# Up-projection of a feed-forward layer: plain weight blocks split by ScalarE and VectorE, and three plain pairs in place of four ahead of the seven-product pairs

## The chip, the cores and the metric

One core of a Trainium2 chip runs the whole program. The metric is device time in microseconds (us), the median of the runs of one kernel. Its engines work side by side, each through its own queue in order, and meet at semaphores: TensorE (PE) multiplies, VectorE (DVE), ScalarE (ACT) and GpSimd (POOL) work elementwise, SyncE (SP) issues the DMA transfers.

## The reference

Two layers of a model with 1024 channels over 1040 positions (16 meta tokens and 1024 tokens). The change lies in the feed-forward part of the first:

```
xn = rms_norm(h, ffn_pre_g)                       # 1024 channels
gu = xn @ w_up                                    # 1024 x 5632
g  = causal_dwconv(gu[..., :2816], w, b)          # 3 taps
f  = (gelu(g) * gu[..., 2816:]) @ w_down          # 2816 -> 1024
h  = h + rms_norm(f, ffn_post_g)
```

All of it is float32. The columns of `w_up` are cut into 22 blocks of 128 gate columns and 22 of 128 up columns; a gate block and its up block are a pair.

## The kernel before

**Numbers.** Every float32 factor is split into two float16 parts, high and low; weights are first multiplied by 64 (`WSCALE`). One product is three matmuls: high by high, high by low, low by high. To split a weight block of 128x1024 means to make `hi = f16(64 w)` and `lo = 64 w - hi`.

**The phase.** `ffn_up_phase` makes the 22 pairs. The first `PLAIN` = 4 are plain: the gate block (even number b, buffer slot 0) and the up block (odd, slot 1) are each multiplied over three token tiles of 342 and eight blocks of channels, 72 matmuls a block, into banks 0 to 2 and 3 to 5 of PSUM. The first two blocks are made ahead; their last token tile waits for the norm that ends the phase before. The other `WINO` = 18 pairs take seven products of half the size instead of eight (Strassen's scheme in Winograd's form), over two token parts of 257 and 256: 7 x 2 x 4 x 3 = 168 matmuls a pair. These need sums of the input blocks, T1 to T4, and sums of the weight blocks, S1 to S4.

**The input sums.** They are made while the plain pairs run, in eight rounds (`T_ROUNDS`), one after another through the same four float32 buffers. A round r is: four additions on POOL (`whole_inputs(r)`, L2191), which wait until the round before has been split; four differences on DVE (`t_differences(r)`, L2469); four casts to the high part on ACT (`t_highs(r)`, L2351); four subtractions for the low part on DVE (L2472). The second product of the first seven-product pair needs all rounds.

**The plain weight blocks** from number 2 on: SP loads one when the slot's last low part is made; ACT multiplies it by 64 in place (`weight_scaled`, L2333), ACT casts it to the high part (`weight_high`, L2357), POOL subtracts (`low_part`, L2179). PE starts a block when its low part is there (`L.cut`) and its PSUM banks are emptied (`L.emptied`).

**A plain pair q after its matmuls:** ACT copies the gate banks out (L2387), DVE convolves (three instructions, L2483 to L2485), ACT takes the gelu (L2372), DVE multiplies by the up banks (L2514, semaphore `s_f`, which empties them), ACT and DVE split the result (`f_high`, L2377; `f_low`, L2491).

**The order** on each engine is written out by hand. In the loop over the four plain pairs DVE has: a round, the convolution, another round, the multiplication by the up banks, `f_low`. For the last plain pair the first two weight quarters of seven-product pair 0 take the place of the second round: ACT makes `high(0, "A11")` and `high(0, "A12")` (L2368), DVE the low parts (L2476). PE's order for seven-product pair 0 is the product of A11 (P1), then a wait for `s_f` of the last plain pair, then the product of A12 (P2), then that of S2 (P6), and four more. POOL makes S1 to S4 (`combine`, L2201 to L2209) after the last round's additions.

After the 22 pairs PE goes on with the down-projection, whose unit u takes PSUM bank `u % 6`.

Of the kernel before, what the change touches and what calls it, by code (L numbers as in the profile page):

```python
# [10 lines left out]
ALU = mybir.AluOpType  # L11
# [238 lines left out]
def done(L, b):  # L250

    return b * L.parts + (L.parts + SLOTS)
# [1811 lines left out]
    return nc.tensor.matmul(out, lo, xhi, start=False, stop=(j == DB - 1))  # L2064


PLAIN = 4
WINO = FFB - PLAIN
SPLITS = ("A11", "A12", "A22", "S1", "S2", "S3", "S4")
PRODUCTS = ("P1", "P2", "P6", "P5", "P7", "P4", "P3")  # L2070
# [4 lines left out]
PART_W = (257, 256)  # L2075
PART_AT = (0, 2 * PART_W[0])
F_STEPS = 2 * PARTS
T_ROUNDS = PARTS * (DB // 2)
Z_PARKED = slice(META, META + 755)
Z_FIRST = slice(META, F0 + 2 * FT)  # L2080
Z_LAST = slice(F0 + 2 * FT, META + 755)
# [2 lines left out]
def ffn_up_phase(nc, S, L, Ld, hs, ssq, rows, parked_z):  # L2084
# [3 lines left out]
    with Phase(nc) as ctx:  # L2088
# [32 lines left out]
        s_hi, s_lo = ({n: sem(f"{n}_{part}") for n in SPLITS} for part in ("hi", "lo"))  # L2121
        s_p = sem("wino_products")
        s_p1, s_u2, s_u3, s_c11, s_c12, s_c22 = (sem(n) for n in ("p1", "u2", "u3", "c11", "c12", "c22"))
        s_zp, s_whole, s_whigh, s_third = sem("z_parked"), sem("weights_scaled"), sem("weights_high"), sem("third_part")
        half = lambda x, i: x[:, i * BANK:(i + 1) * BANK]
        s32 = {"A11": half(L.raw[:, 0, :], 0), "A12": half(L.raw[:, 0, :], 1), "A21": half(L.raw[:, 1, :], 0), "A22": half(L.raw[:, 1, :], 1),
               "S1": half(rows, 0), "S2": half(rows, 1), "S3": half(L.raw[:, 0, :], 0), "S4": half(L.raw[:, 0, :], 1)}
# [8 lines left out]
        with nc.Block() as block:  # L2136
# [36 lines left out]

            @block.gpsimd
            def _(pool):
                def low_part(b):
                    s = b % SLOTS
                    pool.wait_ge(s_whigh, b - SLOTS + 1)
                    nc.gpsimd.tensor_tensor(L.lo[:, s, :], L.raw[:, s, :], L.hi[:, s, :], ALU.subtract).then_inc(L.cut, 1)  # L2179

                def whole_inputs(r):
                    e, j = divmod(r, DB // 2)
                    if r == 0:
                        pool.wait_ge(C.summed, 1)
                    else:
                        pool.wait_ge(s_tlo, 4 * r)
                    if r == DB // 2:
                        pool.wait_ge(C.low, DB)
                        pool.wait_ge(s_zp, 32)
                    for t, (k, h) in zip(temps_of(r), ((j, 1), (j, 0), (j + DB // 2, 1), (j + DB // 2, 0))):  # L2190
                        nc.gpsimd.tensor_tensor(t, S.xhi[:, k, x_at(e, h)], S.xlo[:, k, x_at(e, h)], ALU.add).then_inc(s_tsum, 1)  # L2191

                def combine(i):
                    pool.wait_ge(s_in["U"], 16 * (i + 1))
                    pool.wait_ge(s_in["A11"], 16 * (i + 1))
                    if i == 0:
                        pool.wait_ge(s_tlo, 4 * (DB // 2))
                    else:
                        pool.wait_ge(s_lo["S1"], i)
                        pool.wait_ge(s_lo["S2"], i)  # L2200
                    nc.gpsimd.tensor_tensor(s32["S1"], s32["A21"], s32["A22"], ALU.add).then_inc(s_comb, 1)  # L2201
                    pool.wait_ge(s_comb, 4 * i + 1)
                    nc.gpsimd.tensor_tensor(s32["S2"], s32["S1"], s32["A11"], ALU.subtract).then_inc(s_comb, 1)
                    pool.wait_ge(s_comb, 4 * i + 2)
                    pool.wait_ge(s_lo["A11"], i + 1)
                    nc.gpsimd.tensor_tensor(s32["S3"], s32["A11"], s32["A21"], ALU.subtract).then_inc(s_comb, 1)
                    pool.wait_ge(s_in["A12"], 16 * (i + 1))
                    pool.wait_ge(s_lo["A12"], i + 1)
                    nc.gpsimd.tensor_tensor(s32["S4"], s32["A12"], s32["S2"], ALU.subtract).then_inc(s_comb, 1)  # L2209

                for b in range(SLOTS, SLOTS * PLAIN):
                    whole_inputs(b - SLOTS)
                    if b == SLOTS * PLAIN - 1:
                        whole_inputs(b - SLOTS + 1)
                    low_part(b)
                whole_inputs(T_ROUNDS - 1)
                for i in range(WINO):
                    combine(i)
                pool.wait_ge(s_p, free(WINO - 1, "A12"))
                cut_first(nc, S, pool, Ld, 1)  # L2220
                pool.wait_ge(s_p, free(WINO - 1, "A22"))
                cut_first(nc, S, pool, Ld)

            @block.tensor
            def _(pe):
# [87 lines left out]
                for part in range(PARTS_AHEAD):  # L2313
                    k0, k1 = DOWN_PARTS[part]
                    pe.wait_ge(Ld.cut, part + 1)
                    pe.wait_ge(s_flo, 2 * k1)
                    for k in range(k0, k1):
                        hi, lo = (x[:, part, (k - k0) * P:(k - k0 + 1) * P] for x in (Ld.hi, Ld.lo))
                        fhi, flo = (x[0][:, k, :] for x in (S.f_hi, S.f_lo))
                        out = S.ps[:, 0, :]  # L2320
                        nc.tensor.matmul(out, hi, fhi, start=(k == 0), stop=False)
                        nc.tensor.matmul(out, hi, flo, start=False, stop=False)
                        nc.tensor.matmul(out, lo, fhi, start=False, stop=False)

            @block.scalar
            def _(act):
                nc.scalar.sem_inc(L.emptied, SLOTS)
                nc.scalar.preload_act_table_set("natural_log_exp_and_others")

                def weight_scaled(b):  # L2330
                    s = b % SLOTS
                    act.wait_ge(L.landed[s], 16 * (b // SLOTS + 1))
                    nc.scalar.activation(L.raw[:, s, :], L.raw[:, s, :], ACT.Copy, scale=WSCALE).then_inc(s_whole, 1)  # L2333

                link_root(nc, S, act, C, 0, DB)
                for k in range(DB):
                    link_square(nc, act, C, k)
                weight_scaled(2)
                link_root(nc, S, act, C, 1, DB)
                for k in range(DB):  # L2340
                    link_high(nc, act, C, k)
# [10 lines left out]

                def weight_high(b):
                    s = b % SLOTS
                    act.wait_ge(s_whole, b - SLOTS + 1)
                    act.wait_ge(L.products, b + 1)
                    nc.scalar.activation(L.hi[:, s, :], L.raw[:, s, :], ACT.Copy).then_inc(s_whigh, 1)  # L2357

                def high(i, name):
                    if name[0] == "A":  # L2360
# [20 lines left out]

                for q in range(PLAIN):
                    if q:
                        t_highs(2 * q + (q + 1 == PLAIN))
                    act.wait_ge(L.products, done(L, q * 2))
                    act.wait_ge(s_conv, q)
                    nc.scalar.activation(fm(raw[:, :]), psum_tn(S, 0)[:, :, 0:FT], ACT.Copy, scale=1.0 / WSCALE).then_inc(s_raw, 1)  # L2387
# [2 lines left out]
                    if q + 1 < PLAIN:  # L2390
                        weight_high(2 * q + 2)
                    if q == 0:
                        t_highs(0)
                        weight_scaled(3)
                        weight_high(3)
                    elif q + 1 < PLAIN:
                        weight_scaled(2 * q + 3)
                    if q + 1 == PLAIN:
                        for name in ("A11", "A12"):
                            high(0, name)  # L2400
                    gelu(q)
                    if q + 1 < PLAIN:
                        t_highs(2 * q + 1)
                    if q + 2 < PLAIN:
                        weight_scaled(2 * q + 4)
                    if q + 1 == PLAIN:
                        for name in ("S1", "S2"):
                            high(0, name)
# [2 lines left out]
                    if 0 < q < PLAIN - 1:  # L2411
                        weight_high(2 * q + 3)
                    f_high(q)
                    if q + 2 == PLAIN:
                        t_highs(2 * q + 2)
                for i in range(WINO):
                    q = PLAIN + i
                    for e in range(PARTS):
# [35 lines left out]
            def _(dve):  # L2454
# [19 lines left out]
                def low(i, name):  # L2474
                    dve.wait_ge(s_hi[name], i + 1)
                    nc.vector.scalar_tensor_tensor(w16[1][name], s32[name], WSCALE, w16[0][name], ALU.mult, ALU.subtract).then_inc(s_lo[name], 1)  # L2476
# [19 lines left out]
                def gated(i, q):  # L2496
                    dve.wait_ge(s_gelu, q + 1)
                    for e in range(PARTS):
                        dve.wait_ge(s_p, made(i, "P4", e))
                        for h, (of, scale) in enumerate(((bank_a(i, e), 1.0 / WSCALE), (c22[e], 1.0))):  # L2500
                            nc.vector.scalar_tensor_tensor(f_at(acc, e, h), of, scale, f_at(acc, e, h), ALU.mult, ALU.mult).then_inc(s_f, 1)

                for q in range(PLAIN):
                    t_differences(2 * q + (q + 1 == PLAIN))
                    dve.wait_ge(s_raw, q + 1)
                    convolve(q)
                    if q + 1 < PLAIN:
                        t_differences(2 * q + 1)
                    else:
                        low(0, "A11")  # L2510
                        low(0, "A12")
                    dve.wait_ge(L.products, done(L, q * 2 + 1))
                    dve.wait_ge(s_gelu, q + 1)
                    nc.vector.scalar_tensor_tensor(fm(acc[:, :]), psum_tn(S, 1)[:, :, 0:FT], 1.0 / WSCALE, fm(acc[:, :]),  # L2514
                                                   ALU.mult, ALU.mult).then_inc(s_f, F_STEPS)
                    if q + 1 == PLAIN:
                        for name in ("S1", "S2"):
                            low(0, name)
                    f_low(q)
                    if q + 2 == PLAIN:  # L2520
                        t_differences(2 * q + 2)
                for name in ("S3", "A22", "S4"):
                    low(0, name)
                for i in range(WINO):
# [81 lines left out]
def ffn_down_phase(nc, S, A, Lz, Ld, L, down, ssq, parked_h, s_parked_h, parked_z):  # L2606
# [7 lines left out]
    with Phase(nc) as ctx:  # L2614
# [21 lines left out]
        with nc.Block() as block:  # L2636
# [24 lines left out]
            def _(pe):  # L2661
                f_of = lambda parts, k, r: parts[2][:, k, :] if r else parts[k // F_KEPT][:, k % F_KEPT, :]

                def part(u, q):
                    i = LOAD_OF[u, q]
                    at, w = toks(u).start, width(u)
                    out = S.ps[:, u % 6, 0:w]
                    k0, k1 = DOWN_PARTS[q]
                    pe.wait_ge(s_cut, i + 1)
                    for k in range(k0, k1):  # L2670
# [28 lines left out]
            def _(act):  # L2699
# [9 lines left out]
                def evac(u):  # L2709

                    act.wait_ge(s_pr, NQ * u + NQ)
                    w = width(u)
                    ps = S.ps[:, u % 6, 0:w]
                    nc.scalar.activation(down[:, DOWN_UNITS[u][0], toks(u)], ps, ACT.Copy, scale=1.0 / WSCALE)
                    if not new_sum(u) and u >= 2:
                        act.wait_ge(s_acc, sums_by(u - 2))
# [1522 lines left out]
```

## Time and profile before

| | |
|---|---|
| median of 3 runs | 2248.89 us (2245.49 to 2254.71) |
| profiled execution | 2248.3 us, of it the span of the trace 2246.5 us |
| mean granted TensorE clock | 0.989 of full speed |
| PE busy | 2141.7 us, 95% of the span |
| DVE, ACT, POOL busy | 1577.0 us (70%), 1008.3 us (45%), 631.7 us (28%) |
| plain blocks 2 to 7 on PE | from 953.79 us to 1020.5 us of the span |
| seven-product pairs on PE | from 1025.80 us to 1359.97 us |

In the rows of a timeline the first number is the start in us from the start of the span, the second the time from the first start to the last end; x3 says that three like instructions are merged. In brackets stand the idle time of the engine before it and what ended it. A matmul's own duration is a model (they overlap); the distance of two starts is what PE takes for one.

### The profile page before, as it was taken

To read this page: it belongs to the slowest core of one execution; us is meant where nothing else is said; L and a number is where in the kernel's file an instruction comes from. 1 tells how busy PE (TensorE), PEld (TensorE's weight loads), DVE (VectorE), ACT (ScalarE), POOL (GpSimd) and SP (SyncE) were. 2 spreads that over 40 slices of the span, in tenths; PEclk is the share of its full clock that TensorE was granted. 3 is DMA by queue.
4 is the path that set the end of the run, shared out by engine and by line. 5 is a ranking of instruction groups with operands and counts; after the bars stand their busy time and mean duration, and the time that the engine had idled before them with its cause. 6 is when DMAs were issued, how large, how long until landed. Compare 5 with 4: busy or idle time off the path is not lost. (4 is left out here: it accounts for less than half of the span.)

```text
span 2246.5 us, 45705 instructions
## 1 busy us (share of the span) xinstructions
PE 2141.7 (95%) x19060; PEld 1435.6 (64%) x19060; DVE 1577.0 (70%) x2075; ACT 1008.3 (45%) x1778; POOL 631.7 (28%) x405
## 2 busy tenths in 40 slices
PE   7999999999999899898999999999999999989998
PEld 4666665556666566567888885458644445578847
DVE  7966888988888656777888884257687675236654
ACT  3227776666666444544444443235553332224321
POOL 4556763200011120053333321000155532101160
PEclk9999999999999999999999999999999999999999
DMA  3113213777777521211111115326433522033412
GB/s 137 48 47 105 85 63 84 138 139 147 143 137 148 135 100 63 100 44 64 58 57 57 58 43 184 103 71 211 131 99 118 177 91 89 11 99 100 169 62 76
DMA packets 292085, 224.25 MB, mean 100 GB/s; under 512 B 205536, under 2 KB 255904, under 8 KB 290480
## 3 DMA queue, kind: packets, MB, share of 16 engines
q1 hardware_dynamic: 291888, 221.44, 35.5%
q8 instruction: 146, 2.39, 0.4%
q14 instruction: 51, 0.42, 0.1%
HBM read 148.46 MB, written 28.86 MB: 79 GB/s over the span
## 5 line engine op out<-in xcount | busy, mean ns | idle before, releaser
L1543 DVE TENSOR_TENSOR_SCAN att_left<-att_left,att_unseen_prefix 16x16 f32<-16x16 f32 (+5 forms) x144 | 183.5, 1275 | 35.0 <-ACT att_left L1382 35.0
L3027 PE MATMUL ps<-second_x_hi,whi_z 128*128 128x512 f16 (+1 forms) x480 | 178.8, 372 | 3.4 <-POOL wlo_z L2992 1.9
L1276 PE MATMUL ps<-x_hi,whi_z 128*128 128x348 f16 x560 | 175.6, 314 | 3.4 <-DVE att_q L1487 3.4
L3029 PE MATMUL ps<-second_x_hi,wlo_z 128*128 128x512 f16 (+1 forms) x480 | 178.5, 372 | 0.0
L3028 PE MATMUL ps<-second_x_lo,whi_z 128*128 128x512 f16 (+1 forms) x480 | 178.5, 372 | 0.0
L1278 PE MATMUL ps<-x_hi,wlo_z 128*128 128x348 f16 x560 | 174.6, 312 | 0.0
L1277 PE MATMUL ps<-x_lo,whi_z 128*128 128x348 f16 x560 | 174.4, 311 | 0.0
L2992 POOL TENSOR_TENSOR wlo_z<-wraw_z,whi_z 128x1024 f16<-128x1024 f32 x28 | 65.8, 2348 | 180.0 <-ACT whi_z L3220 180.0
L1502 DVE SCALAR_TENSOR_TENSOR att_left_split<-att_left,att_left_split 128x256 f16<-128x256 f32 (+7 forms) x128 | 107.0, 836 | 7.4 <-ACT att_left_split L1396 7.3
L1382 ACT ACTIVATE att_left<-ps 16x16 f32<-16x16 f32 (+5 forms) x144 | 86.1, 598 | 39.7 <-PE ps L1292 39.5
L1396 ACT ACTIVATE att_left_split<-att_left 128x256 f16<-128x256 f32 (+7 forms) x128 | 86.7, 678 | 36.2 <-DMA att_left_turned<-att_left_split 29.4
L3220 ACT ACTIVATE whi_z<-wraw_z 128x1024 f16<-128x1024 f32 x28 | 29.6, 1056 | 132.4 <-PE ps L3029 117.3
L1323 PE MATMUL ps<-att_left_turned,att_v_tokens 128*64 128x128 f16 x1728 | 63.4, 227 | 25.7 <-DMA att_left_turned<-att_left_split 18.2
L1234 POOL CAST att_v_meta_split<-att_v_meta 32x128 f16<-32x128 f32 x8 | 9.2, 1152 | 277.4 <-ACT att_v_meta L1388 277.4
L3027 PEld LDWEIGHTS ps<-second_x_hi,whi_z 128*128 128x128 f16 x480 | 46.9, 98 | 62.5 <-issue 6.3
L2254 PE MATMUL ps<-x_hi,whi_z 128*128 128x257 f16 (+1 forms) x288 | 79.1, 275 | 5.3 <-DVE wlo_z L2476 5.3
L1323 PEld LDWEIGHTS ps<-att_left_turned,att_v_tokens 128*64 128x64 f16 x1728 | 53.3, 114 | 44.4 <-issue 34.8
L1276 PEld LDWEIGHTS ps<-x_hi,whi_z 128*128 128x128 f16 x560 | 54.5, 97 | 42.1 <-issue 14.7
L3028 PEld LDWEIGHTS ps<-second_x_lo,whi_z 128*128 128x128 f16 x480 | 47.0, 98 | 53.4 <-issue 3.6
L219 PE MATMUL ps<-x_hi,whi_xbc 128*128 128x348 f16 x240 | 74.6, 311 | 6.8 <-DVE x_lo L529 5.9
L3029 PEld LDWEIGHTS ps<-second_x_hi,wlo_z 128*128 128x128 f16 x480 | 47.0, 98 | 53.2
L2255 PE MATMUL ps<-x_lo,whi_z 128*128 128x257 f16 (+1 forms) x288 | 79.0, 274 | 0.0
(695 smaller groups left out, 6703.6 us busy)
## 6 DMA issues: line engine op xcount, KB each, us to landing
wraw_z<-in_w_second SPq DMA_DIRECT2D x30, 512.0 KB, 3.6
wraw_z<-in_w_up SPq DMA_DIRECT2D x26, 512.0 KB, 3.6
wraw_z<-in_w_qkv SPq DMA_DIRECT2D x24, 512.0 KB, 4.5
wraw_z<-in_w_down SPq DMA_DIRECT2D x20, 512.0 KB, 3.7
raw_down<-in_w_down SPq DMA_DIRECT2D x20, 512.0 KB, 3.5
seg<-dt_a_sums SPq DMA_DIRECT2D x18, 512.0 KB, 5.1
wraw_z<-in_w_up SPq DMA_DIRECT2D x36, 256.0 KB, 2.5
second_work<-parked_units SPq DMA_DIRECT2D x7, 1280.0 KB, 6.0
```

The costliest lines, as they stand in the source:

```text
L1276: nc.tensor.matmul(lin_ps(g), hi, xhi, start=(kb == 0), stop=False)
L1277: nc.tensor.matmul(lin_ps(g), hi, xlo, start=False, stop=False)
L1278: last = nc.tensor.matmul(lin_ps(g), lo, xhi, start=False, stop=(kb == DB - 1))
L1323: nc.tensor.matmul(o_ps(n)[half(a)], vt[:, t.p % 2, (NSTEP - 1) * (x + 1) - t.j + m, half(a)], turned[t.slot][:, keys_at(t, a) + y * t.j + ...
L1382: nc.scalar.activation(of_head(t, a, 0, t.wide), z_ps(a)[0:t.rows, 0:t.wide], ACT.Sigmoid, scale=-0.125).then_inc(s_keep, 1)
L1396: last = nc.scalar.activation(left_part(e, 0, P * t.j), of_head(t, a, 0, P * t.j), ACT.Copy, scale=PSCALE)
L1502: last = nc.vector.scalar_tensor_tensor(low_, of_head(t, a, 0, P * t.j), PSCALE, high, ALU.mult, ALU.subtract)
L1543: nc.vector.tensor_tensor_scan(x, x, unseen, 1.0, ALU.mult, ALU.max).then_inc(s_scan, 1)
L2254: nc.tensor.matmul(out, hi, xhi, start=first and j == 0, stop=False, skip_group_check=True)
L3027: nc.tensor.matmul(out, hi, xhi, start=(j == 0), stop=False)
L3028: nc.tensor.matmul(out, hi, xlo, start=False, stop=False)
L3029: return nc.tensor.matmul(out, lo, xhi, start=False, stop=(j == DB - 1))
```

## The change

It does four things. (1) `PLAIN` is 3 and `WINO` 19. (2) The split of plain blocks moves: ACT makes `hi = f16(64 raw)` in one instruction, DVE makes `lo = 64 raw - hi` in one (`plain_low`); the scaling in place and POOL's subtraction are gone. (3) The eight rounds are spread over three plain pairs by the table `T_AT`: for each pair what comes ahead of the convolution, what after it, and what after `f_low`. (4) The PSUM banks of the down-projection are turned by two when `WINO` is odd.

```diff
-PLAIN = 4
+PLAIN = 3
 WINO = FFB - PLAIN
...
+def down_bank(u):
+    return (u + 2 * (WINO % 2)) % 6
+
+
 T_ROUNDS = PARTS * (DB // 2)
+T_AT = (((0,), (1,), (2,)), ((3,), (4,), (5,)), ((6,), (7,), ()))
...
@@ block.gpsimd
-                for b in range(SLOTS, SLOTS * PLAIN):
-                    whole_inputs(b - SLOTS)
-                    if b == SLOTS * PLAIN - 1:
-                        whole_inputs(b - SLOTS + 1)
-                    low_part(b)
-                whole_inputs(T_ROUNDS - 1)
+                for r in range(T_ROUNDS):
+                    whole_inputs(r)
...
@@ block.scalar
                 def weight_high(b):
                     s = b % SLOTS
-                    act.wait_ge(s_whole, b - SLOTS + 1)
+                    act.wait_ge(L.landed[s], 16 * (b // SLOTS + 1))
                     act.wait_ge(L.products, b + 1)
-                    nc.scalar.activation(L.hi[:, s, :], L.raw[:, s, :], ACT.Copy).then_inc(s_whigh, 1)
+                    nc.scalar.activation(L.hi[:, s, :], L.raw[:, s, :], ACT.Copy, scale=WSCALE).then_inc(s_whigh, 1)
...
                 for q in range(PLAIN):
                     if q:
-                        t_highs(2 * q + (q + 1 == PLAIN))
+                        for r in T_AT[q][0]:
+                            t_highs(r)
...
                     if q == 0:
-                        t_highs(0)
-                        weight_scaled(3)
+                        for r in T_AT[q][0]:
+                            t_highs(r)
                         weight_high(3)
-                    elif q + 1 < PLAIN:
-                        weight_scaled(2 * q + 3)
...
                     gelu(q)
-                    if q + 1 < PLAIN:
-                        t_highs(2 * q + 1)
-                    if q + 2 < PLAIN:
-                        weight_scaled(2 * q + 4)
+                    for r in T_AT[q][1]:
+                        t_highs(r)
...
@@ block.vector
+                def plain_low(b):
+                    s = b % SLOTS
+                    dve.wait_ge(s_whigh, b - SLOTS + 1)
+                    nc.vector.scalar_tensor_tensor(L.lo[:, s, :], L.raw[:, s, :], WSCALE, L.hi[:, s, :], ALU.mult, ALU.subtract).then_inc(L.cut, 1)
+
                 for q in range(PLAIN):
-                    t_differences(2 * q + (q + 1 == PLAIN))
+                    for r in T_AT[q][0]:
+                        t_differences(r)
+                    if q + 1 < PLAIN:
+                        plain_low(2 * q + 2)
                     dve.wait_ge(s_raw, q + 1)
                     convolve(q)
-                    if q + 1 < PLAIN:
-                        t_differences(2 * q + 1)
-                    else:
+                    if q == 0:
+                        plain_low(3)
+                    if q + 1 == PLAIN:
                         low(0, "A11")
                         low(0, "A12")
+                    for r in T_AT[q][1]:
+                        t_differences(r)
                     dve.wait_ge(L.products, done(L, q * 2 + 1))
                     dve.wait_ge(s_gelu, q + 1)
                     nc.vector.scalar_tensor_tensor(fm(acc[:, :]), psum_tn(S, 1)[:, :, 0:FT], 1.0 / WSCALE, fm(acc[:, :]),
                                                    ALU.mult, ALU.mult).then_inc(s_f, F_STEPS)
+                    if 0 < q < PLAIN - 1:
+                        plain_low(2 * q + 3)
...
                     f_low(q)
-                    if q + 2 == PLAIN:
-                        t_differences(2 * q + 2)
+                    for r in T_AT[q][2]:
+                        t_differences(r)
```

## Rows read from the trace of the kernel before

**Rows 1.** The page, busy time by engine (share of the span, instructions)

```profile
PE 2141.7 (95%) x19060; PEld 1435.6 (64%) x19060; DVE 1577.0 (70%) x2075; ACT 1008.3 (45%) x1778; POOL 631.7 (28%) x405
```

**Rows 2.** Who PE waited for, 1026 to 1365 us: total, times, longest

```profile
PE ps L2254 <- ACT mixed_squares L2380: 0.4, 1, 0.4
```

**Rows 3.** Timeline of PE at the seams of the phase

```profile
952.26 0.31 PE L2064 MATMUL ps<-x_hi,wlo_z 128*128 128x342 f16 x1
953.79 0.31 PE L219 MATMUL ps<-x_hi,whi_z 128*128 128x342 f16 x1 [1.22 <-POOL wlo_z L2179]
...
964.10 0.31 PE L221 MATMUL ps<-x_hi,wlo_z 128*128 128x342 f16 x1
966.39 0.32 PE L219 MATMUL ps<-x_hi,whi_z 128*128 128x342 f16 x1 [1.99 <-ACTq L2410]
...
1020.18 0.31 PE L221 MATMUL ps<-x_hi,wlo_z 128*128 128x342 f16 x1
1025.80 0.37 PE L2254 MATMUL ps<-x_hi,whi_z 128*128 128x257 f16 x1 [5.31 <-DVE wlo_z L2476]
...
1029.70 0.27 PE L2254 MATMUL ps<-x_hi,whi_z 128*128 128x257 f16 x1
...
1046.11 0.27 PE L2254 MATMUL ps<-x_hi,whi_z 128*128 128x257 f16 x1
...
1359.97 0.38 PE L2321 MATMUL ps<-second_x_hi,whi_z 128*128 128x512 f16 x1
```

**Rows 4.** Busy time of PE by stretch: length, busy, granted clock, DMA

```profile
968.00:970.00 2.00, 2.00 (x9) 0.50 0.00 0
...
1026.00:1028.00 2.00, 2.00 (x11) 0.50 0.01 4
```

**Rows 5.** Timeline of DVE, 920 to 1026 us

```profile
920.81 1.22 DVE L1989 SCALAR_TENSOR_TENSOR wlo_z<-wraw_z,whi_z 128x1024 f16<-128x1024 f32 x1
...
951.78 2.15 DVE L2472 TENSOR_TENSOR t<-mixed_squares,t 128x257 f16<-128x257 f32 x1 [1.49 <-ACT t L2351]
...
954.86 0.80 DVE L2483 TENSOR_SCALAR gate_conv<-gate_raw,params 128x1024 f32<-128x1024 f32 x1
...
957.31 1.58 DVE L2485 SCALAR_TENSOR_TENSOR gate_conv<-gate_raw,params,gate_conv 128x1024 f32<-128x1024 f32 x1
...
965.07 1.22 DVE L2514 SCALAR_TENSOR_TENSOR gate_conv<-ps,gate_conv 128x1026 f32<-128x1026 f32 x1
...
967.68 1.16 DVE L2491 TENSOR_TENSOR f_lo_other<-gate_conv,f_hi_other 128x512 f16<-128x512 f32 x1
968.77 1.34 DVE L2469 TENSOR_TENSOR mixed_squares<-mixed_squares 128x257 f32<-128x257 f32 x3
...
971.49 0.42 DVE L2472 TENSOR_TENSOR t<-down_squares,t 128x257 f16<-128x257 f32 x1
...
1016.40 3.34 DVE L2469 TENSOR_TENSOR mixed_squares<-mixed_squares 128x256 f32<-128x256 f32 x3 [2.66 <-POOL z L2191]
...
1021.12 0.42 DVE L2472 TENSOR_TENSOR z<-z 128x256 f16<-128x256 f32 x1
1021.60 0.81 DVE L2483 TENSOR_SCALAR gate_conv<-gate_raw,params 128x1024 f32<-128x1024 f32 x1
...
1024.97 1.28 DVE L2476 SCALAR_TENSOR_TENSOR wlo_z<-wraw_z,whi_z 128x512 f16<-128x512 f32 x2
```

**Rows 6.** Timeline of POOL, 951 to 1020 us

```profile
951.51 2.13 POOL L2179 TENSOR_TENSOR wlo_z<-wraw_z,whi_z 128x1024 f16<-128x1024 f32 x1 [22.77 <-ACT whi_z L2357]
955.02 4.40 POOL L2191 TENSOR_TENSOR mixed_squares<-x_hi,x_lo 128x257 f32<-128x257 f16 x3 [1.38 <-DVE t L2472]
959.38 0.67 POOL L2191 TENSOR_TENSOR down_squares<-x_hi,x_lo 128x257 f32<-128x257 f16 x1
...
1013.81 1.92 POOL L2191 TENSOR_TENSOR mixed_squares<-x_hi,x_lo 128x256 f32<-128x256 f16 x3 [4.28 <-DVE z L2472]
...
1016.32 1.26 POOL L2201 TENSOR_TENSOR down_squares<-wraw_z 128x512 f32<-128x512 f32 x1
```

**Rows 7.** Timeline of ACT, 970 to 974 us

```profile
970.93 1.01 ACT L2387 ACTIVATE gate_raw<-ps 128x1026 f32<-128x1026 f32 x1
972.11 1.06 ACT L2357 ACTIVATE whi_z<-wraw_z 128x1024 f16<-128x1024 f32 x1 [0.17 <-ACT gate_raw L2387]
```

More of the change, by code:

```diff
@@ L2123, in ffn_up_phase @@
         s_p1, s_u2, s_u3, s_c11, s_c12, s_c22 = (sem(n) for n in ("p1", "u2", "u3", "c11", "c12", "c22"))
-        s_zp, s_whole, s_whigh, s_third = sem("z_parked"), sem("weights_scaled"), sem("weights_high"), sem("third_part")
+        s_zp, s_whigh, s_third = sem("z_parked"), sem("weights_high"), sem("third_part")
         half = lambda x, i: x[:, i * BANK:(i + 1) * BANK]
@@ L2175, in _ @@
             def _(pool):
[L2176 to L2179, printed above, removed]
                 def whole_inputs(r):
@@ L2319, in _ @@
                         fhi, flo = (x[0][:, k, :] for x in (S.f_hi, S.f_lo))
-                        out = S.ps[:, 0, :]
+                        out = S.ps[:, down_bank(0), :]
                         nc.tensor.matmul(out, hi, fhi, start=(k == 0), stop=False)
@@ L2328, in _ @@
                 nc.scalar.preload_act_table_set("natural_log_exp_and_others")
[L2330 to L2333, printed above, removed]
                 link_root(nc, S, act, C, 0, DB)
@@ L2337, in _ @@
                     link_square(nc, act, C, k)
-                weight_scaled(2)
                 link_root(nc, S, act, C, 1, DB)
@@ L2413, in _ @@
                     f_high(q)
-                    if q + 2 == PLAIN:
-                        t_highs(2 * q + 2)
+                    for r in T_AT[q][2]:
+                        t_highs(r)
                 for i in range(WINO):
@@ L2519, in _ @@
                     f_low(q)
-                    if q + 2 == PLAIN:
-                        t_differences(2 * q + 2)
+                    for r in T_AT[q][2]:
+                        t_differences(r)
                 for name in ("S3", "A22", "S4"):
@@ L2666, in part @@
                     at, w = toks(u).start, width(u)
-                    out = S.ps[:, u % 6, 0:w]
+                    out = S.ps[:, down_bank(u), 0:w]
                     k0, k1 = DOWN_PARTS[q]
@@ L2712, in evac @@
                     w = width(u)
-                    ps = S.ps[:, u % 6, 0:w]
+                    ps = S.ps[:, down_bank(u), 0:w]
                     nc.scalar.activation(down[:, DOWN_UNITS[u][0], toks(u)], ps, ACT.Copy, scale=1.0 / WSCALE)
```

## The prediction

> **What bounds the kernel now.** I read the page first: PE is busy for 95% of the span [rows 1], so time is won where PE has less to do or stops waiting, and nowhere else. The question is then how near PE each part of this phase runs. The waits of PE during the seven-product pairs answer for these: one of 0.4 us in more than 300 us [rows 2]. So they run at PE's pace, and their price is a distance of starts: from the second pair's first matmul at 1046.11 to the end at 1359.97 are 313.86 us for 17 pairs, 18.46 us a pair, 0.1099 us for each of 168 matmuls [rows 3]. A plain block is 72 matmuls; block 2 runs from 953.79 and issues its last at 964.10, which is 71 steps of 0.1452 us [rows 3]: 10.46 us a block, 20.9 us a pair.
>
> The timeline of PE at the seams shows where it stands still between 952.6 and 1026 us: 1.22 us ahead of block 2, for POOL's low part; 1.99 us ahead of block 3, for its PSUM banks, which ACT hands over after DVE's multiplication; 5.31 us ahead of seven-product pair 0, for DVE's low part of A11 [rows 3]. The stretches of clock say what follows the longer two: the granted clock is 0.50, the 1.2 GHz level, at 968 to 970 and at 1026 to 1028 us [rows 4]. Blocks 3 to 7 take from 966.39 to 1020.33 (the last start and a step), 53.9 us where five blocks at full clock are 52.3: 1.6 us lost. The product of A11 takes from 1025.80 to 1029.70, 3.90 us where 24 x 0.1099 = 2.64 are due: 1.26 us lost [rows 3].
>
> The last of those waits tells who sets the pace here. It isn't PE: it is the chain of rounds on POOL and DVE, with the convolutions between them. That chain has eight rounds to fit whether there are four plain pairs or three, and the timelines of DVE and POOL price its links.
>
> - A round on DVE with POOL quiet or nearly so: 968.77 to 971.91, 3.15 us. The last round, beside POOL's first sum of weights: 1016.40 to 1021.54, 5.1 us [rows 5].
> - The four additions on POOL: 1013.81 until the next instruction at 1016.32, 2.55 us; beside a convolution 955.02 to 960.05, 5.0 us [rows 6].
> - A convolution: 1021.60 until the low parts at 1024.97, 3.4 us; beside the additions 954.86 to 958.89, 4.0 us [rows 5].
> - The multiplication 1.2 us; `f_low` 1.8 us with the wait of 0.8 us ahead of it left out (the second half is seen stretched to 1.16); a low part of 128x1024 on DVE, in the phase before, 1.22 us [rows 5].
> - ACT: the copy of the gate banks starts 2.16 us after the start of a round that stands ahead of it, the high part of the next block 1.18 us after the copy, for 1.06 us [rows 5, 7].
>
> **The change part by part.**
>
> *The pair.* One plain pair, 20.9 us of PE, becomes one seven-product pair, 18.46 us: 2.5 us less on PE. SP moves the same bytes for it. The bank turn of the down-projection adds no instruction.
>
> *ACT.* Six scalings and two high parts fall away. ACT is idle for much of this stretch, so this is worth something only at one place: block 4's high part, which now needs no scaling ahead of it. Nothing on PE waits for that today. I take 0.
>
> *POOL.* Six subtractions go, 2.1 us or more each (951.51, 2.13 us) [rows 6]. They lengthened the chain in two ways. They kept POOL from the next additions, and they held DVE: its L2472 that began at 951.78 took 2.15 us, ending at 953.93 just after POOL's 953.64, where the like one at 971.49 took 0.42 [rows 5, 6].
>
> *DVE.* Four low parts come in, 4 x 1.22 us, all on the chain. What they do shows only in order, so I walk it, from 948.48 us, where DVE starts round 0 in both kernels:
>
> 1. Round 0 is free of POOL: the low parts follow ACT's casts, end 953.15 (954.94 before). Low part of block 2: 954.4. PE starts block 2 at 954.55, 0.75 us later than before.
> 2. Convolution 0 beside round 1's additions: 958.4. Low part of block 3: 959.65. Round 1: 962.9. Multiplication: 964.2. PE ends block 2 at 965.0 and goes straight on: the wait of 1.99 us and its slow clock (1.6 us) are gone.
> 3. Wait 0.8 and `f_low` 1.8: 966.8. Round 2: 969.95. Round 3's additions start only now and DVE has nothing else in its queue: 972.55. Round 3: starts there; the copy of gate 1 is queued behind its casts on ACT, 972.55 + 2.16 + 1.18 + 1.06 = 976.95 for block 4's high part, low part at 978.25. PE ends block 3 at 975.5 and starts block 4 at 978.4: a **new wait of 2.9 us**, perhaps with a slow clock after it.
> 4. Convolution 1 (its additions mostly done, 3.7): 981.95. Round 4: 985.1. Multiplication: 986.3. High part 5 on ACT and low part on DVE: 988.7. PE ends block 4 at 988.9 and meets it with 0.2 us in hand. `f_low`: 990.0. Round 5: 993.15. Additions of round 6, again with nothing beside them: 995.75. Round 6 and the copy behind its casts: 999.0.
> 5. PE ends block 5 at 999.3, or at about 1001 if the clock fell in step 3. That doesn't matter: convolution 2, 4.0 us, ends at 1003.0 and the low part of A11 at 1003.7. PE starts pair 0 at 1003.85, after a wait of 4.5 us (5.31 before), again at the low clock: A11 ends at 1007.75.
> 6. Here is the second new wait. The low part of A12 ends at 1004.3, and round 7 now stands **between it and the multiplication of the last plain pair**, while POOL already combines weights, as it did beside the last round before: 5.1 us, 1009.4. Multiplication: 1010.6. PE, which needs these banks for A12, starts it at 1010.75 and has waited 3.0 us. The copies, S1, S2 and `f_low` are queued behind it on ACT and DVE, and come in time for S2's product 2.6 us later.
>
> The sum goes by the start of A12's product, since from there on the pairs run as before: 1010.75 + 18.46 for the added pair = 1029.21, against 1029.70 [rows 3]: 0.5 us less. Laid out by terms: PE's work 2.5 and the old losses 1.22 + 1.99 + 1.6 + 5.31 + 1.26 = 11.4 are paid back by new ones of 2.0 (ahead of block 2) + 2.9 + 4.5 + 1.26 + 3.0 = 13.7; these differ by 0.2, from rounding of the steps (0.3 us). The profiled execution took 2248.3 us, so 2247.8; it lies 0.6 us under the median of the three, and I forecast **2248.4 us**.
>
> **Bounds of what I had to choose.** The convolutions could all run at 3.4 us (0.6, 0.3 and 0.6 less) and round 7 at 3.15 (1.95 less): A12 at 1007.75, where A11's own end holds it anyway, 3.5 us better than before in all. Or the additions hold DVE in full: see the second rival. I take the stretched values where the same two instructions stood beside each other in the trace, the plain ones elsewhere. A low part on DVE beside additions isn't shown; between 1.22 and 1.22 plus one addition of 0.64 (2.55 over four), I take 1.25. At steps 3 and 6 the clock may or may not fall: nothing at step 3, since step 5 absorbs it; at step 6 up to the 1.6 us seen after the wait at 966.39.
>
> The Trainium skill, page "SBUF — State Buffer", section "Who interferes with whom", says that a VectorE instruction with two SBUF inputs and a GpSimd instruction that reads SBUF exclude each other, the later one being blocked until the first ends. It speaks against this change, which puts four more such instructions on VectorE. By row 951.78 the trace agrees where POOL's instruction is long; by the convolution at 954.86, which lost 0.6 us beside the additions, VectorE loses less than the additions' length. The sum above would by the rule in full be that of the second rival.
>
> **The rivals.**
>
> *The chain runs clean (chance 0.20).* POOL's subtractions were what stretched DVE, and with them gone everything runs at its short value: 3.5 us better, 2245.4 us. For it: the round at 968.77 is short. Against: the last round took 5.1 us beside the sums of weights, which stay.
>
> *POOL's additions hold DVE (0.22), the other side.* In three places additions are due while DVE works on the chain: after rounds 0, 3 and 6. DVE can lose their whole 2.55 us each time, in place of the 0.6, 0.3 and 0.6 I counted: 6.2 us more, so 5.7 us slower than before, 2254.6 us. It decides once more than 0.5 us beyond my values is lost. For it: 951.78. Against: 954.86. A second slow clock at step 6 would lie in the same range.
>
> *No round hides its additions (0.04).* If the additions of rounds 1, 2, 4, 5 and 7 ended late enough for DVE to wait 2.55 us for each, as it does for 3 and 6, 12.8 us come on top: 2261 us. Against it: additions stretched to 5.0 us still end inside what DVE has to do meanwhile in rounds 1, 4 and 7.
>
> *PE sets the pace (0.02).* The change would then do what a count of matmuls says, and all waits but the one ahead of block 2 vanish: block 5 ends at 954.55 + 41.8 = 996.4, A12 starts at 999.0, 11.7 us better than my sum: 2236.7 us. It needs the chain 12 us shorter.
>
> **How the numbers follow.** My forecast, within 2.5 us either way, has 0.50; 0.02 is left for what I don't see, in the stages behind this one. The likely cases lie from 2245.4 to 2254.6; the three runs of before lie 3.4 under and 5.8 over their median, so a median may be off by some 2 to 3 us. The range is 2242 to 2257. A change of 0.5% is 11.2 us, about what a measurement of this kernel tells from none; only the last two rivals and the unseen reach it: faster 0.03, slower 0.05, the same 0.92.
>
> **What the profile after would show.** Right: PE's wait for PSUM banks ahead of block 3 gone; a wait of 2 to 4 us ahead of block 4, for DVE's low part; pair 0 starting at 1003 to 1005 us and A12's product 6 to 8 us behind it, with DVE's multiplication as releaser; 313.9 + 18.5 us from the second pair to the end. Wrong: block 4 starting without a wait (then ACT or the rounds are faster than I count), A12 behind A11 at once, or rounds on DVE of 4 us and more where only additions run on POOL. The forecast fails as a whole if the later phases move, which nothing in the diff touches but the bank turn.

## The result: 0.4% slower, where no measurable change was forecast

| | median, us | lowest to highest | ratio to before, 95% interval |
|---|---|---|---|
| before | 2248.82 (7 runs) | 2245.49 to 2254.71 | |
| changed | 2256.96 (7 runs) | 2253.57 to 2260.88 | 1.0038 [1.0026, 1.0051] |

The forecast of 2248.4 us is 8.6 us too low. The time lies at the very edge of the range of 2242 to 2257, and it moved the other way, by 8.1 us. The profiled execution of the changed kernel took 2260.88 us (span 2259.1), 3.9 us over its median.

Matched instruction by instruction with the trace of before, the 12.6 us by which its span is longer fall in four places: 6.5 us ahead of the up-projection, 2.8 us in it and the hand-over to the next phase, 0.8 us less from there up to 2114 us, and 4.1 us near 2120 us. The first and the last lie in code that the diff doesn't touch.

The busy time of the engines, from the page (share, instructions), answers to [rows 1]:

```profile
PE 2149.6 (95%) x19084; PEld 1442.5 (64%) x19084; DVE 1580.5 (70%) x2095; ACT 1004.8 (44%) x1782; POOL 627.9 (28%) x403
```

Who PE waited for, 920 to 1400 us, with total, times and longest:

```profile
PE ps L219 <- DVE wlo_z L2493: 5.0, 2, 3.0
PE ps L2250 <- DVE gate_conv L2511: 4.3, 1, 4.3
PE ps L2250 <- DVE wlo_z L2463: 4.0, 1, 4.0
...
PE ps L2672 <- DVE wlo_down L2751: 2.3, 1, 2.3
```

The same waits in the timeline of PE (start, time, the wait ahead in brackets), for [rows 3]: block 2, block 4, A11's product, A12's product.

```profile
961.02 0.31 PE L219 MATMUL ps<-x_hi,whi_z 128*128 128x342 f16 x1 [1.93 <-DVE wlo_z L2493]
...
985.10 0.45 PE L219 MATMUL ps<-x_hi,whi_z 128*128 128x342 f16 x1 [3.03 <-DVE wlo_z L2493]
...
1011.55 0.27 PE L2250 MATMUL ps<-x_hi,whi_z 128*128 128x257 f16 x1 [4.02 <-DVE wlo_z L2463]
...
1020.29 0.40 PE L2250 MATMUL ps<-x_hi,whi_z 128*128 128x257 f16 x1 [4.28 <-DVE gate_conv L2511]
```

The wait for PSUM banks ahead of block 3 is gone, and the waits that were forecast stand where they were forecast (the 5.0 us above are the 1.93 ahead of block 2 and the 3.03 ahead of block 4). The last is longer: 4.28 us, not 3.0. The clock by stretch of 2 us (length, busy, granted clock, DMA), for [rows 4], is low after each of the two last waits, and for longer after the second (it was low for a stretch after the 3.03 us as well, 0.52 at 986 to 988 us):

```profile
1012.00:1014.00 2.00, 2.00 (x11) 0.50 0.00 0
...
1022.00:1024.00 2.00, 2.00 (x11) 0.50 0.00 0
```

DVE at the end of the plain pairs, for [rows 5]: the low part of block 3; those of A11 and A12; round 7 from its differences to its last low part; the multiplication.

```profile
965.10 1.70 DVE L2493 SCALAR_TENSOR_TENSOR wlo_z<-wraw_z,whi_z 128x1024 f16<-128x1024 f32 x1
...
1010.25 2.83 DVE L2463 SCALAR_TENSOR_TENSOR wlo_z<-wraw_z,whi_z 128x512 f16<-128x512 f32 x2
1013.00 4.29 DVE L2456 TENSOR_TENSOR mixed_squares<-mixed_squares 128x256 f32<-128x256 f32 x3
...
1018.68 0.42 DVE L2459 TENSOR_TENSOR z<-z 128x256 f16<-128x256 f32 x1
1019.01 1.22 DVE L2511 SCALAR_TENSOR_TENSOR gate_conv<-ps,gate_conv 128x1026 f32<-128x1026 f32 x1
```

POOL meanwhile, for [rows 6]: the last addition for round 7, and without a pause the four sums of weight blocks, which end at 1017.0.

```profile
1009.21 1.65 POOL L2191 TENSOR_TENSOR z<-x_hi,x_lo 128x256 f32<-128x256 f16 x1
1010.82 1.71 POOL L2201 TENSOR_TENSOR down_squares<-wraw_z 128x512 f32<-128x512 f32 x1
1012.61 1.59 POOL L2203 TENSOR_TENSOR down_squares<-down_squares,wraw_z 128x512 f32<-128x512 f32 x1
1014.28 1.33 POOL L2206 TENSOR_TENSOR wraw_z<-wraw_z 128x512 f32<-128x512 f32 x1
1015.57 1.44 POOL L2209 TENSOR_TENSOR wraw_z<-wraw_z,down_squares 128x512 f32<-128x512 f32 x1
```

From 1010.25 to 1017.0 the two engines run side by side, and what takes 1.28 us alone [rows 5] takes 2.83; the round takes 6.1 us (1013.00 to 1019.10) where I had 5.1.

### The profile page after: what moved, and what is told of

Same layout as the page of the kernel before. It is cut to its first block and busy times, and to the rows that moved or that the text cites. A ratio compares the mean times of both kernels' runs of the same rounds, so it can differ in the third digit from the quotient of the medians.

```text
span 2259.1 us, 45803 instructions
## 1 busy us (share of the span) xinstructions
PE 2149.6 (95%) x19084; PEld 1442.5 (64%) x19084; DVE 1580.5 (70%) x2095; ACT 1004.8 (44%) x1782; POOL 627.9 (28%) x403
## 5 line engine op out<-in xcount | busy, mean ns | idle before, releaser
L2250 PE MATMUL ps<-x_hi,whi_z 128*128 128x256 f16 (+1 forms) x304 | 84.8, 279 | 8.3 <-DVE gate_conv L2511 4.3
L2251 PE MATMUL ps<-x_lo,whi_z 128*128 128x256 f16 (+1 forms) x304 | 84.8, 279 | 0.0
L2252 PE MATMUL ps<-x_hi,wlo_z 128*128 128x256 f16 (+1 forms) x304 | 84.7, 279 | 0.0
L1276 PEld LDWEIGHTS ps<-x_hi,whi_z 128*128 128x128 f16 x560 | 54.5, 97 | 42.0 <-issue 14.7
```

The lines of the kernel that those rows point to most:

```text
L1276: nc.tensor.matmul(lin_ps(g), hi, xhi, start=(kb == 0), stop=False)
L2250: nc.tensor.matmul(out, hi, xhi, start=first and j == 0, stop=False, skip_group_check=True)
```

## The experiments

All times in this table count from DVE's first difference of round 0, so that what comes ahead drops out. Block 2, A11, A12 and S2 are the starts of these products on PE, "end" is the first matmul of the down-projection.

| kernel | median, us | ratio, 95% interval | block 2 | A11 | A12 | S2 | end |
|---|---|---|---|---|---|---|---|
| before | 2248.8 | | 5.3 | 77.3 | 81.2 | 83.9 | 411.5 |
| changed | 2257.0 | 1.0038 [1.0026, 1.0051] | 6.0 | 56.6 | 65.3 | 70.4 | 416.0 |
| before again | 2248.6 | 0.9996 [0.9986, 1.0006] | 5.3 | 77.3 | 81.3 | 83.9 | 411.5 |
| changed again | 2257.0 | 1.0032 [1.0020, 1.0044] | 6.0 | 56.6 | 65.3 | 70.1 | 415.6 |
| split alone, 4 pairs | 2239.7 | 0.9957 [0.9945, 0.9970] | 6.0 | 68.8 | 71.4 | 74.1 | 402.8 |
| 3 pairs, old split | 2264.9 | 1.0076 [1.0063, 1.0089] | 5.3 | 62.9 | 71.6 | 76.7 | 422.4 |
| changed, 163 waits more | 2252.2 | 1.0017 [1.0008, 1.0027] | 6.0 | 56.5 | 65.3 | 70.4 | 415.9 |
| split alone, 93 waits more | 2244.0 | 0.9979 [0.9967, 0.9990] | 6.0 | 68.8 | 71.4 | 74.0 | 402.2 |
| changed, rounds spread | 2259.9 | 1.0046 [1.0029, 1.0063] | 6.0 | 50.8 | 55.5 | 67.6 | 415.5 |
| changed, weight sums late | 2258.3 | 1.0049 [1.0031, 1.0066] | 6.0 | 56.6 | 61.3 | 65.3 | 416.4 |
| split alone, low part first | 2239.6 | 0.9951 [0.9934, 0.9967] | 4.4 | 68.8 | 71.4 | 74.1 | 403.0 |
| split, 5 pairs | 2241.2 | 0.9963 [0.9949, 0.9977] | 6.0 | 89.6 | 92.2 | 94.9 | 404.0 |

**The two kernels once more**, unchanged.

> The kernel before, once more. Theory A (the loss beyond the up-projection in the profiled execution, 6.5 us ahead of it and 3.3 us behind it, is chance of that execution): ratio 1.000 within 0.2%, and two executions of this same kernel differ by some us in the stretch from 700 to 800 us and behind 2100 us. Theory B (those stretches belong to the changed program): the seams outside the up-projection repeat within 1 us.

> The changed kernel, once more. Theory A: the up-projection costs 2.8 us more than before again, the stretches outside it come out otherwise than in the first profile (+6.5 and +3.3 us), and the median lies 3 to 5 us over before. Theory B: +6.5 us ahead of the phase and +3.3 us behind it again, median 8 us over before.

Neither theory holds as a whole. The 6.5 us ahead of the phase were chance: this time the changed kernel comes to the phase 0.9 us earlier than before again. (In the first profile of the changed kernel PE stood still for 2.8 us in the attention stage, ahead of L1326, for nothing that the profile names, and the clock was low for longer behind it.) The loss near 2120 us came again. This pair of traces has 2.6 us in the phase and its hand-over, 0.7 from there up to 2114 us, and 4.4 near 2120; less the 0.9 us ahead of the phase that is 6.8 us, the distance of the two spans (2251.6 and 2244.7). In this execution the clock stayed high after the wait of 3.0 us ahead of block 4; the wait ahead of A11 is longer for it (5.1 us, not 4.0), and A11 starts at 56.6 all the same.

**The two halves of the change apart.** The split alone:

```diff
-PLAIN = 3
+PLAIN = 4
-T_AT = (((0,), (1,), (2,)), ((3,), (4,), (5,)), ((6,), (7,), ()))
+T_AT = (((0,), (1,), ()), ((2,), (3,), ()), ((4,), (5,), (6,)), ((7,), (), ()))
```

> Four plain pairs as before, with the new split by ScalarE and VectorE (rounds: 0, 1 / 2, 3 / 4, 5, 6 / 7, as before). Theory 1 (the split is a gain, the loss is in the three pairs with eight rounds): from VectorE's start of round 0 to A12's product 77 to 80 us, against 81.2 before, so 1 to 4 us less. Theory 2 (the split is what costs, since its low parts stand in VectorE's queue on the chain): 82 to 85 us, 1 to 4 us more.

The pairs alone, taken from the changed kernel:

```diff
                 for r in range(T_ROUNDS):
                     whole_inputs(r)
+                    if r in (0, 1, 3, 4):
+                        low_part({0: 2, 1: 3, 3: 4, 4: 5}[r])
...
-                    if q + 1 < PLAIN:
-                        plain_low(2 * q + 2)
```

(with `weight_scaled` back on ScalarE at its places, and the other two calls of `plain_low` gone as well).

> Three plain pairs with the rounds of the change, and the old split (scaling in place on ScalarE, subtraction on GpSimd after rounds 0, 1, 3 and 4). Theory 1 (the three pairs with eight rounds cost): from VectorE's round 0 to A12's product 66 to 70 us, which with 18.46 us for the added pair is 3 to 7 us over the 81.2 of before. Theory 2 (the split costs): 62 to 63 us, no more than before.

They are opposites. The split gains 9.2 us of median (2239.65 against 2248.82) and 8.7 us in the phase; on top of it, three pairs in place of four cost 17.3 us of median and 13 us in the phase (415.6 and 416.0 against 402.8); most of the rest is the stop near 2120 us, which the split alone does not have. With the old split three pairs reach A12 at 71.6, later than I allowed. What PE waits for in the split alone, 950 to 1400 us:

```profile
PE ps L2672 <- DVE wlo_down L2751: 2.3, 1, 2.3
PE ps L219 <- DVE wlo_z L2493: 1.9, 1, 1.9
PE ps L2250 <- ACT mixed_squares L2370: 1.5, 1, 1.5
```

Between block 2 and A11's product PE waits for nothing: 68.8 less 6.0 is 62.8, six blocks of 10.46.

**The stop near 2120 us.** PE's waits marked "issue" (for nothing that the profile shows) from 2100 to 2140 us, in before again:

```profile
PE ps L3746 <- issue: 0.2, 1, 0.2
```

and in changed again:

```profile
PE ps L3731 <- issue: 2.4, 1, 2.4
...
PE ps L3716 <- issue: 0.5, 1, 0.5
```

The stretches of 2 us in changed again, with the granted clock and the share and rate (GB/s) of DMA behind the busy time, show it at the tail of a stretch of heavy DMA, with the clock at 0.50, the 1.2 GHz level, after it:

```profile
2121.00:2123.00 2.00, 2.00 (x80) 1.00 1.14 492
2123.00:2125.00 2.00, 0.76 (x31) 1.00 0.74 302
2125.00:2127.00 2.00, 0.87 (x9) 0.71 0.40 125
2127.00:2129.00 2.00, 2.00 (x19) 0.50 0.06 16
```

Instructions come by DMA too; the page of the changed kernel has a queue for them (packets, MB, share of 16 engines):

```profile
q8 instruction: 147, 2.41, 0.4%
```

That is 16 KB a transfer. In the steady stretch of the seven-product pairs 22 of them start between 1063.49 and 1347.61 us in before again, 13.53 us apart on the average. A pair of 18.46 us has 349 instructions on PE (168 matmuls, 168 weight loads, 13 waits of their own), so a transfer carries 349 x 13.53 / 18.46 = 256. The fourth plain pair was a pass of a loop and added none; the nineteenth seven-product pair adds 349, one transfer and 93 instructions. So the borders between transfers lie elsewhere in all that follows. The test adds waits (two lines at a product make one instruction more: the traces have 163 and 93 more than without) for semaphores reached long before, without any effect on the order:

```diff
+PAD = 163
...
                     pe.wait_ge(s_lo[name], i + 1)
+                    if len(padded) < PAD:
+                        padded.append(name)
+                        pe.wait_ge(s_raw, 1)
+                        pe.wait_ge(s_gelu, 1)
```

> The changed kernel with 163 waits more on TensorE, all of them for semaphores that have long been reached, spread over the seven-product pairs. Theory F (instruction supply: the changed kernel carries 349 instructions more on TensorE, 256 make one transfer of 16 KB, and the remainder of 93 moves a transfer into the busy stretch near 2120 us, where TensorE stands still for 2.4 us and its clock falls): 93 + 163 is one whole transfer, so the stop near 2120 us goes and the median is 3.5 to 5 us lower than the changed kernel's. Theory C (the stop is chance): no more than 1 us of difference, and the stop comes as often as before.

> The new split with four plain pairs (which has no stop near 2120 us) with 93 such waits more on TensorE. Theory F: the stop of some 2.4 us appears, with a slow clock after it, and the median is 3.5 to 5 us over that of the split alone, so near 2244 us. Theory C: within 1 us of 2239.7.

Both came out as instruction supply has it. With 163 more the changed kernel is 4.8 us faster (2252.18 against 2256.96); with 93 more the split alone is 4.3 us slower (2243.98 against 2239.65), and the phase itself moved by no more than 0.6 us in either. What is left of "issue" in the same stretch, with 163 waits more:

```profile
PE ps L3752 <- issue: 0.9, 1, 0.9
```

and in the split alone with 93 more (2090 to 2140 us), where there was none before:

```profile
PE ps L3738 <- issue: 2.9, 1, 2.9
```

The Trainium skill, page "Runtime: NRT & Kernel Launch", section "Instruction fetch mechanics", says that the stream of instructions is refilled in blocks of 16 KiB, 256 instructions, and that the cost of crossing a border is mostly hidden. The block size agrees with the 256 worked out here; the cost was not hidden in this place, 2.4 us and a slow clock.

The traces of all twelve kernels show the borders themselves. Counted in PE's records (matmuls, weight loads, waits) back from the end of the trace, the stop lies 2258 records before the end in all five traces of kernels with 349 instructions more (2.1 to 2.65 us) and in the split with 93 more. In before, before again and the changed kernel with 163 more a short wait of the same sort (0.8, 0.2 and 0.9 us) lies 2166 records before the end, 92 later. Every other "issue" wait of PE behind 1400 us in these traces lies a multiple of 256 away from these places, to within one; with five plain pairs (349 fewer) the one that there is lies 94 off the place in before, to the other side, and there is no stop. So the stops lie at borders of instruction transfers. Why the same crossing costs 2.1 us and more at one place of the code, and 0.9 us or nothing at the other, is not shown: at the dear place DMA moves 360 to 490 GB/s and PE runs up to 84 short matmuls in 2 us, and no run parts the two.

**Is it the rounds?** The rounds moved so that fewer additions stand bare between them (in the trace VectorE waits for GpSimd's additions ahead of round 5 alone, for 2.67 us):

```diff
-T_AT = (((0,), (1,), (2,)), ((3,), (4,), (5,)), ((6,), (7,), ()))
+T_AT = (((0,), (1,), (2,)), ((), (3,), (4,)), ((5,), (6,), (7,)))
```

> The changed kernel with its rounds placed otherwise: 0, 1, 2 / none, 3, 4 / 5, 6, 7, the last one behind f_low. Theory 1 (the chain of rounds sets the pace, and two of the additions and one convolution stand in its way bare): counted from VectorE's round 0, A11's product starts at 48.5 to 50 us (56.6 in the changed kernel), A12's at 53 to 55 (65.3), S2's at 62 to 64 (67.9), and the phase is 4 to 6 us shorter than the changed kernel's. Rival (TensorE's own work sets it): no change of the phase's length.

A11 and A12 came forward by 5.8 and 9.8 us, a little short of what I expected. (The 67.9 us that this expectation and the next give for S2 are the start of A12's second token part; S2 starts at 70.4 and 70.1 in the changed kernel.) It brought nothing: PE's waits ahead of A11, A12 and S2 in that kernel are

```profile
997.89 0.27 PE L2250 MATMUL ps<-x_hi,whi_z 128*128 128x257 f16 x1 [2.79 <-DVE wlo_z L2463]
...
1002.60 0.28 PE L2250 MATMUL ps<-x_hi,whi_z 128*128 128x257 f16 x1 [1.91 <-DVE gate_conv L2511]
...
1014.74 0.38 PE L2250 MATMUL ps<-h_tile,s_hi 128*128 128x257 f16 x1 [9.34 <-ACT mixed_squares L2370]
```

The wait went on to the first product that needs every round (ACT's copy named there is itself queued behind the last round). The chain does hold PE, but its end is S2, not A12, and it ends 2.5 to 2.8 us earlier only; the phase ends within 0.5 us of the changed kernel's, and the median is 2.9 us higher, for which the phase has no reason.

**Is it the sums of weights beside round 7?**

```diff
                     if i == 0:
-                        pool.wait_ge(s_tlo, 4 * (DB // 2))
+                        pool.wait_ge(s_tlo, 4 * T_ROUNDS)
```

> The changed kernel, in which GpSimd begins the sums of weight blocks only when the last round has been split. Theory P (these sums are what stretched round 7 to 6.05 us and the low parts of A11 and A12 to 2.83 us): the round takes 3.1 to 3.5 us, the two low parts 1.3 to 1.9, A12's product starts at 61 to 62.5 us from round 0 (65.3 in the changed kernel), S2's at 65 to 67 (67.9): 1 to 3 us less in all. Rival (they are long for another reason): A12 at 65 us again, and S2 later by the 2.7 us of the two sums.

The collision is shown. DVE's two low parts and round 7 (differences, last low part) in that kernel:

```profile
1011.13 1.76 DVE L2463 SCALAR_TENSOR_TENSOR wlo_z<-wraw_z,whi_z 128x512 f16<-128x512 f32 x2
1012.82 1.33 DVE L2456 TENSOR_TENSOR mixed_squares<-mixed_squares 128x256 f32<-128x256 f32 x3
...
1015.53 0.42 DVE L2459 TENSOR_TENSOR z<-z 128x256 f16<-128x256 f32 x1
```

3.1 us for the round and 1.76 for the low parts, where there were 6.1 and 2.83. A12 starts 4.0 us earlier and S2 5 us. But the end of the phase did not move forward, it is 0.4 to 0.8 us later, and I had expected 1 to 3 us less. PE's timeline shows where it went:

```profile
1021.12 0.27 PE L2250 MATMUL ps<-h_tile,s_hi 128*128 128x257 f16 x1 [1.17 <-ACT z L2370]
...
1028.09 0.28 PE L2250 MATMUL ps<-h_tile,s_hi 128*128 128x257 f16 x1 [1.53 <-ACT mixed_squares L2370]
...
1033.03 0.32 PE L2250 MATMUL ps<-t,whi_z 128*128 128x257 f16 x1 [2.13 <-ACT mixed_squares L2370]
```

Three waits inside pair 0 for ACT's copies, and a low clock from 1033.1 to 1036.6 us. The first copy is queued behind ACT's split of the late sums, the other two behind its splits for the next pair, which had waited 4.36 us for the weights to land and 1.88 us for their sum. In the changed kernel there is none of the three.

**Who sets the pace with four pairs?** The low part of block 2 ahead of round 0's:

```diff
                         nc.vector.tensor_tensor(now[out], now[x], now[y], ALU.subtract).then_inc(s_tdiff, 1)
+                    if r == 0:
+                        plain_low(SLOTS)
...
-                    if q + 1 < PLAIN:
+                    if q and q + 1 < PLAIN:
                         plain_low(2 * q + 2)
```

> The new split with four plain pairs, and the low part of block 2 on VectorE right after the differences of round 0, ahead of that round's low parts. Theory 1 (there are two limits that meet: TensorE's own work and the chain on VectorE, which is 0.35 us short of it at A11): TensorE starts block 2 at 4.3 to 4.7 us from VectorE's round 0 (6.02 in the split alone), but A11's product still at 68.3 to 68.6 (68.79), with a wait of about 1.3 us ahead of it: the phase gains under 0.5 us. Rival (TensorE alone sets the pace): all 1.5 us come through to the end of the phase.

Block 2 starts 1.7 us earlier, A11 at 68.8 as before. The waits of PE in it, 950 to 1400 us, hold 1.4 of the 1.7 us that were gained at block 2:

```profile
PE ps L219 <- ACTq L2397: 1.1, 1, 1.1
PE ps L2250 <- DVE wlo_z L2470: 0.3, 1, 0.3
```

Most went into a wait for PSUM banks ahead of block 3, not ahead of A11 as I had said. Two limits meet here.

**One plain pair more.**

```diff
-PLAIN = 4
+PLAIN = 5
-T_AT = (((0,), (1,), ()), ((2,), (3,), ()), ((4,), (5,), (6,)), ((7,), (), ()))
+T_AT = (((0,), (1,), ()), ((2,), (3,), ()), ((4,), (5,), ()), ((6,), (7,), ()), ((), (), ()))
```

> The new split with five plain pairs and 17 seven-product pairs (rounds 0, 1 / 2, 3 / 4, 5 / 6, 7 / none). Theory 1 (with the split, TensorE's work alone sets the length at four plain pairs and more, and a plain pair costs 2.46 us more than a seven-product pair): the phase is 2.2 to 2.8 us longer than with four, 405.0 to 405.6 us from round 0, and TensorE waits for nothing between block 2 and pair 0. Rival (the chain of rounds still holds TensorE at four pairs): less than 1.5 us longer, or shorter. The number of TensorE's instructions falls by 349, so by the theory of instruction supply the stretch near 2120 us may come out otherwise as well.

A11 comes 20.8 us later, PE's full price of a plain pair; with 18.46 back that is 2.3 us. The phase became 1.2 us longer, less than forecast and by the rival's bound: the wait inside pair 0 fell from 1.5 to 0.4 us, so ACT's copy, which is queued behind the weight sums of the next pair, was late there even with four pairs.

## Why the prediction was wrong, step by step

- **Steps 1 to 5 were right.** In the changed kernel the low part of block 2 ends 5.9 us after the start of round 0 (5.9 by my walk), round 3 starts at 24.3 (24.1), block 4's low part ends at 30.0 (29.8), round 5 ends at 45.0 (44.7), convolution 2 at 55.3 (54.5), with waits of 3.03 us ahead of block 4 (2.9) and 4.02 ahead of A11 (4.5). The wait ahead of block 3 is gone.
- **Step 6 was right in its mechanism and too small.** The low parts of A11 and A12 next to the additions and POOL's sums of weights took 2.83 us, not 1.28, and round 7 took 6.1, not 5.1. With the 0.7 us lost up to the end of convolution 2, A12 starts at 65.3, 3.0 us later than the 62.3 of my walk. I took round 7's price from a trace where only two of the four sums stood beside it [rows 5, 6], and gave the low parts none. This is the second rival, POOL holding DVE, at half of its price and for the most part in another place: around and after the last additions, not in three places.
- **The clock at step 6 was left out of the sum.** It was low over A12's product as well; from A12 to the end the pairs took 350.7 and 350.3 us (416.0 and 415.6 less 65.3) where 411.5 - 81.2 + 18.46 = 348.8 was due, 1.6 to 1.9 us more. I had it as a bound of 1.6. My 0.5 us of gain, with 3.0 and 1.7 against it, makes the 4.2 us that were measured (411.5 to 415.6 and 416.0).
- **The statement that nothing behind the phase is touched but the bank turn was wrong**, and this is as large a part: 4.1 and 4.4 us near 2120 us. The 349 instructions of the added pair shift the borders of instruction transfers, and one falls where PE then stands still for 2.1 and 2.4 us, in a stretch where DMA is busy. No rival of mine had this, though the page gives the queue.
- Against both stands 1.5 us: the low clock at the start of the down-projection, which is there in before (0.55 of full speed at 1373 to 1375 us) and in before again, is missing in both traces of the changed kernel, and in that of the split alone; the reason stays open.
- **The sign of the whole** follows from the halves. I costed ACT's and POOL's parts of the split at what they did to the chain, but never asked what the split does by itself with four pairs: there its 8.7 us all come through. Of the old kernel's 11.4 us at waits and their slow clock it leaves 1.9 us ahead of block 2, and adds 1.5 us inside pair 0, for which there were 0.4. I let the same gain be eaten by the shorter cover of three pairs, which was right, and lost sight of it.
- **What the measurement tells** was set too coarsely: I took 11.2 us as about the least that shows, but the interval is 0.13% either way, and 8.1 us are clear of it.

Open stays some 0.4 to 2 us of the 8.1 us between the medians, which these pairs of traces do not place, and why the spread of the two variants with moved rounds and sums is larger (2252.68 to 2265.48, and 2254.11 to 2268.69). That POOL and DVE hold one another through a shared port was not tried by itself; what is shown is that with the sums out of the way DVE's round has its short time.

The version to keep is the split with four plain pairs: 2239.65 us, 0.4% faster than before and 0.8% faster than the changed kernel. Its variant with the low part first measures the same.

## What to carry to other kernels

A preparation of fixed length (here eight rounds, about 64 us) needs that much cover; taking away cover that looks dearer on TensorE (20.9 against 18.46 us) pays only while TensorE is the one that sets the pace, and moving single waits about then only hands them to the next product. Take a change of two halves apart before judging it: one half was worth 9 us, the other cost 17, of it some 4 by the stop near 2120 us. And count the instructions that an unrolled piece adds on the engine that bounds the kernel, for they change where instruction transfers fall in everything behind. That can cost or save some 4 us without any merit of the change itself.

## What the runs showed of the hardware that I had not expected

TensorE can stand still at a border of its instruction transfers: for 2.4 and 2.9 us at the end of a stretch of DMA at 360 to 490 GB/s, with the clock at 1.2 GHz behind it, 4.3 and 4.8 us of the median, moved in and out by 93 or 163 instructions placed more than 700 us earlier. At other borders it lost 1.1 us or less. And two of DVE's low parts of 128x512 took 1.28 us with GpSimd idle, 1.76 beside the end of an addition, and 2.83 beside that and a sum of weights.
